# GLA scores, level of 16 tokens: four 16x16 blocks in the square in place of one 128x64 product of its own

## The reference, cut to what matters

```python
def step(s, blk):                       # one chunk of tokens, 4 heads, dk=128, dv=256
    b = jnp.cumsum(gc, axis=1)          # gc: log of the forget gate, per key channel
    diff = b[:, :, None] - b[:, None, :]
    w = jnp.exp(jnp.where(causal[None, :, :, None, None], diff, -jnp.inf))
    scores = jnp.einsum('bihd,bjhd,bijhd->bhij', qc, kc, w)
    o = jnp.einsum('bhij,bjhe->bihe', scores, vc) + jnp.einsum('bihd,bhde->bihe', qc * jnp.exp(b), s)
```

## Time and profile before

| what | value |
|---|---|
| median of 3 runs | 2491.69 us (2489.11 to 2498.32) |
| profiled execution | 2490.22 us, span 2488.4 us |
| PE busy | 2436.4 us, 98% |
| PEld busy | 2386.6 us, 96% |
| DVE busy | 1438.0 us, 58% |
| ACT, POOL busy | 771.0 us, 1044.1 us |
| mean granted PE clock | 0.993 of full |

### The profile page before, as it was taken

The page is one execution under the profiler, slowest core; times in us unless marked ns, Lnnn a source line. Parts: engine busy times, 40 slices in busy tenths (PEclk is TensorE's granted clock), DMA queues, the critical chain, the costliest instruction groups (busy, mean ns, idle before and its releaser), DMA issues. The chain is left out here.

```text
span 2488.4 us, 40883 instructions
## 1 busy us (share of the span) xinstructions
PE 2436.4 (98%) x15934; PEld 2386.6 (96%) x15934; DVE 1438.0 (58%) x2082; ACT 771.0 (31%) x1222; POOL 1044.1 (42%) x773
## 2 busy tenths in 40 slices
PE   8999999999999999999999999999999999999998
PEld 8999999999999999999889889899999999999997
DVE  6974356345545544566767776756445545545576
ACT  4711442223223222223233453441222222222233
POOL 2343224354565465474212112224354554564571
PEclk9999999999999999999989999999999999999999
DMA  4123031111111111113101111131111111111112
GB/s 148 35 62 95 19 125 43 43 52 43 52 43 43 52 52 43 43 52 115 61 18 62 43 45 45 52 117 51 43 43 43 52 43 52 52 43 43 52 51 81
DMA packets 40010, 140.08 MB, mean 56 GB/s; under 512 B 6209, under 2 KB 9921, under 8 KB 38561
## 3 DMA queue, kind: packets, MB, share of 16 engines
q1 hardware_dynamic: 32192, 104.55, 13.1%
q10 hardware_dynamic: 7648, 33.04, 3.6%
HBM read 120.46 MB, written 14.88 MB: 54 GB/s over the span
## 5 line engine op out<-in xcount | busy, mean ns | idle before, releaser
L702 PE MATMUL PS<-RB,WH 128*128 128x384 f32 (+1 forms) x4368 | 1085.3, 330 | 6.3 <-issue 6.3
L702 PEld LDWEIGHTS PS<-RB,WH 128*128 128x128 f32 x4368 | 770.7, 188 | 15.5 <-issue 12.5
L702 PE MATMUL PS<-RA,WH 128*128 128x272 f32 (+2 forms) x3520 | 771.1, 309 | 11.5 <-DVE RA L1787 10.3
L702 PE MATMUL PS<-RB,WL 128*128 128x384 f32 (+1 forms) x2232 | 730.1, 327 | 0.0
L619 POOL TENSOR_TENSOR WH<-WR,FEW 128x1024 fp32r<-128x1024 f32 x128 | 247.0, 1930 | 1118.3 <-PE PS L702 1093.7
L702 PEld LDWEIGHTS PS<-RA,WH 128*128 128x128 f32 x3520 | 588.6, 188 | 16.0 <-issue 11.7
L702 PE MATMUL PS<-RA,WL 128*128 128x272 f32 (+2 forms) x1760 | 541.5, 308 | 0.0
L702 PEld LDWEIGHTS PS<-RB,WL 128*128 128x128 f32 x2232 | 420.1, 188 | 0.0
L622 POOL TENSOR_TENSOR WL<-WR,WH 128x1024 fp32r<-128x1024 f32 x128 | 340.9, 2664 | 10.0
L702 PEld LDWEIGHTS PS<-RA,WL 128*128 128x128 f32 x1760 | 331.5, 188 | 0.0
L1886 DVE TENSOR_TENSOR X<-PS,X 128x544 f32<-128x544 f32 x280 | 202.5, 724 | 203.7 <-PE PS L702 203.7
(11 more groups left out here) (223 smaller groups left out, 2335.0 us busy)
## 6 DMA issues: line engine op xcount, KB each, us to landing
WR<-ws SPq DMA_DIRECT2D x189, 512.0 KB, 3.4
X<-xT ACTq DMA_DIRECT2D x8, 544.0 KB, 7.7
EB<-xT ACTq DMA_DIRECT2D x8, 544.0 KB, 5.5
x_spill<-X ACTq DMA_DIRECT2D x1, 4352.0 KB, 15.8
EB<-x_spill ACTq DMA_DIRECT2D x8, 544.0 KB, 7.0
GA<-st_gla ACTq DMA_DIRECT2D x4, 1024.0 KB, 5.3
glas_o<-GA ACTq DMA_DIRECT2D x4, 1024.0 KB, 5.0
yT<-X SPq DMA_DIRECT2D x16, 208.0 KB, 1.9
```

Of the source, the lines that this page charges most:

```text
L702: return nc.tensor.matmul(out, lhsT, rhs, start=start, stop=stop, skip_group_check=True)
```

## The change

`FINE` goes from 5 to 4. Level 4 (blocks of 32 tokens, halves of 16) now takes the way of levels 5 and 6: four 16x16 blocks at partitions 0, 32, 64 and 96, written over the square, in place of one 128x64 product into columns of its own. The square's mask takes in level 4 and the copy under a mask for it is gone. The mask array is 64 columns narrower. `SPLIT`, which says that level 4 belongs to `A` and not to `A2`, stays 4.

```diff
--- before.py
+++ after.py
@@ -32,7 +32,7 @@
 LT = 4
 LEVELS = 7
-FINE = 5
+FINE = 4
 SPLIT = 4
 SLEVELS = 3
```

## The result

The changed kernel takes 2497.96 us in the median of 11 runs (2494.89 to 2507.88), the kernel before 2491.68 in 11 runs beside it: ratio 1.0033, interval 1.0019 to 1.0048. The medians are 6.3 us apart and the ratio makes it about 8 us: slower, where 5 us less was forecast, and 1 us above the range. The profiled execution has a span of 2497.6 us.

What follows compares the result with a forecast made beforehand. PE, busy for 98% of the span, was taken to bound the kernel, with a few places where DVE is late. -3.5 us (PE) - 1.5 us (DVE) = -5.0 us from 2491.69 gave about 2487 us, range 2480 to 2497.

Steps and rivals of the forecast that it cites:

- The price on PE: Level 4 on PE: 0.21 us a chunk goes, four small blocks cost 0.10, so 32 x 0.11 = 3.5 us less.
- B: Rival on PE: small blocks cost no less than the large product, 0.026 us least per record; 2489 us; chance 0.18.
- C: Rival at the end of item `A`: blocks run one after the other, 0.38 us for four; +5.4 us, 2497; chance 0.08.
- the going over: PE's change to smaller blocks; the price's upper bound counts level 5's pair with it twice, 0.38 us.
- The gain in GLA: Between 1195 and 1640 us: PE's shorter stream and DVE's dropped copy make GLA 3 to 8 us shorter.
- -3.5 - 1.5 = -5.0 us: 3.5 us from PE in 32 chunks, plus 1.5 us in 10 chunks where DVE sets the pace (0.26 for 0.11).
- What lies behind it has the same length: Sign for the profile after: the run behind GLA, from 1640 us, keeps its length.
- the transfer of the masks: Covered at nothing: it is 64 columns narrower and lands over a thousand us before its use.
- rival D: Waits fall differently, so half-clock stretches or DVE operations slowed beside POOL come or go; -5 to +5 us; chance 0.12.
- a difference of more than 10 us in the stretches at half clock: Sign of being wrong: stretches at clock 0.50, 17.1 us in all before, change in length by more than 10 us.
- The chance of 0.93: Whole run: the measured time lies within 0.5% of the kernel before; 0.04 for faster, 0.03 for slower.
- The upper bound of 2497: Upper end of the range: blocks one after the other, or 2487 with two half-clock stretches of 5 us against it.

Runs made afterwards that it cites:

- e1: The changed kernel with 8 idle instructions more on PE, strewn over the projection's groups in GLA: 2489.39 us, ratio 0.9996 to the kernel before.
- e4: The kernel before, with DVE leaving out level 4's copy (those scores are missing) and PE untouched: 2491.81 us, ratio 1.0011 to the kernel before.
- e5: The changed kernel with 8 idle PE instructions more and level 3's copy made twice, so DVE keeps its old length: ratio 1.0009 to the kernel before.
- e2: The kernel before with 128 idle instructions more on PE: 2498.45 us, ratio 1.0037 to the kernel before without them.
- e6: The kernel before with 8 idle PE instructions more, level 4's product left out on PE and level 3's copy made twice: 2491.26 us, ratio 1.0017.
- e7: The changed kernel with PE's two MLP loops written out, so PE never branches back: 2480.72 us, ratio 0.9972 to the kernel before.
- e8: The kernel before with PE's two MLP loops written out: 2480.89 us, ratio 0.9968 to the kernel before.
- e9: As e7, with the fine levels of the fourth chunk of heads 1 to 3 half a projection group later: 2470.82 us, ratio 0.9922 to the kernel before.
- e9b: As e8, with the fine levels of the fourth chunk of heads 1 to 3 half a projection group later: 2480.64 us, ratio 0.9952 to the kernel before.

## Why the prediction was wrong

**The price on PE: right in kind, too high.** I put four blocks at 0.10 us: 0.08 for two rounds of four loads as in the earlier trace rows, and 0.02 on top as my own allowance. No run shows the 0.02; what the runs show in place of the 0.10 is that the blocks added 0.04 us (0.21 - 0.17). The reading of the earlier trace rows, that the loads of several small blocks start side by side, holds. So rivals B and C fall. Of the 0.49 us from the first of the 14 loads of L1108 to the projection's first, 0.26 pass up to the second block's first load (1362.55 to 1362.81, as 1364.10 to 1364.36 before), all twelve loads of the other blocks have started 0.10 us later (by 1362.91), and none starts in the 0.13 us from there to 1363.04. B's least time of 0.026 us a record asks for 0.31 us for these twelve (an estimate, 12 x 0.026). The stretch without a start, which the prediction's bounds and its rival C call the going over, was 0.15 us before (1364.40 to 1364.55), and it stands once in the changed kernel too; what the array does in it no run shows. Behind the 64x64 block no load of L1108 is seen for 0.06 us in the earlier trace rows; between the 32x32 and the 16x16 blocks there is no such stretch. The windows over the loads of L1108 in the changed kernel, to be read against the earlier trace rows, have 8 of them in one 0.04 us and 11 in the next (a load that runs over an edge counts in both):

```profile
1362.82:1362.86 0.04, 0.04 (x8) 1.00 0.00 0
1362.86:1362.90 0.04, 0.04 (x11) 1.00 0.00 0
```

**The gain in GLA: right as a total of the rest, in part by luck.** -3.5 - 1.5 = -5.0 us was the sum. The rest of e1 is 5.4 +- 0.5 us under the kernel before in the same set. With the measured price my own sum would have been 32 x 0.17 + 10 x 0.09 = 6.3 us, so two errors partly cancel. The parts are not those I gave: blocks alone 2.3 (forecast 3.5), copy alone 1.7 (forecast 2.6 for e4), and together 1.4 +- 0.8 more than their sum. If that is more than noise, it fits two engines that take turns as the later one: what one wins alone, the other's lateness eats. The wait for L2387 in the last head shows it: 2.94 us before, 2.67 in e4, 3.07 in e5, 2.80 with both.

**"What lies behind it has the same length": the step that failed.** It was stated as something to check, but the sum held no term for it, and it cost 9 us. The row was there in the kernel before, four waits with 6.3 us in all, and I listed only what lay in GLA:

```profile
PE PS L702 <- issue: 6.3, 4, 1.8
```

The edit's 384 instructions moved all of PE's code behind them, and the place of the second MLP's loop counted. Two waits grew from 1.78 and 1.64 to 4.31 and 4.84 us, and the clock fell behind both (3.4 and 6.8 us at half, at most 5.1 us of cost). The changed kernel's rest is 4.0 us over that of e1 and its clock's cost 5.4 us: 9.4 us between different sets, and 9.2 by the two ratios, 1.0033 and 0.9996. This is shown by e1 and e2, with nothing but idle instructions. (Another step that wasn't covered did no harm: the transfer of the masks isn't over a thousand us ahead of its use. It is issued between 1170 and 1171 us, lands 4.4 us later, and is first used at 1211.5 by L1166, some 36 us on.)

**The clock in GLA, the second step that failed: rival D, right place, wrong shape.** I gave the clock -5 to +5 us as chance with no sign, and the sum nothing. It has a sign: +5.0 +- 1.3 us in e1, +4.6 +- 1.1 in e5, +6.3 +- 1.2 in e6, +4.8 +- 1.7 in e7 against e8. The prediction had named a difference of more than 10 us in the stretches at half clock as a sign of being wrong, and in GLA they grew from 17.1 to 27.3 us. A faster PE in front of a late DVE waits longer at the same places (1.21 us in place of 1.00); that it loses clock for this is the reading that is left. So of the change's 5 us nothing was left, even with the code in a good place (e1, 0.9996). Whether the copy alone (e4, 2.8 +- 1.6 us more) does it too is open, and so is what in these executions, besides the length of the wait, decides on a stretch at half clock.

**The range and the class.** The chance of 0.93 for a change within 0.5% was borne out (0.33%). The upper bound of 2497 held two adverse stretches, and not the longer waits at the branches.

## What to carry to other kernels

Where a program has a hardware loop, count the instructions that an edit puts ahead of it or takes away, and look at the waits for "issue" at the branches before and after: here 9 us in code that wasn't touched were a question of where it lay, and 8 idle instructions ahead of the loop (e1, 0.9996 in place of 1.0033), or the loop written out (e7, 0.9972), settled it. Before making the bound engine faster, look for the waits in which it stands for another engine, and give it work there first: here the same edit was worth no time with these waits in place (e7 against e8) and 7 us or more once two of them were gone (e9 against e9b, 0.9922 against 0.9952). Split each run into the cost of the clock and the rest; the rest told changes of 2 us apart here (its standard error is 0.2 to 0.8 us), where the medians of e1 and of the kernel before hid 5.

## What the runs showed of the hardware that wasn't expected

- Eight idle instructions of PE are worth 8.6 us (2497.96 to 2489.39, ratios to the kernel before of 1.0033 and 0.9996) when they move the start of the second MLP's loop; the branch costs 1.2 to 1.8 us of PE's time in a good place (the shortest 1.23, in e5) and 4.3 to 4.9 in the changed kernel's place and in e2's.
- Four 16x16 fp32 blocks at partitions 0, 32, 64 and 96, behind two 32x32 blocks, add 0.04 us to an item `A` (0.49 us in place of 0.66, of which 0.21 went with level 4's product).
- At one place a wait of PE of 1.2 us in place of 1.0 us went with a stretch of 3.4 us or more at half clock behind it in five profiles of five against none of six; at the same place of the head before, in two of five against none of six. Shortening PE's stream alone raised the clock's cost by 4.6 to 6.3 us (e5, e6).
- Leaving work out on PE (e6) or on DVE (e4) made the kernel no faster: 1.0017 and 1.0011.
